# The intra-chunk product of a bidirectional SSD scan, computed with tokens instead of head channels on the output rows

## The chip, the cores and the metric

The kernel runs on one core of one Trainium2 chip. The metric is the device time of one execution in microseconds. All data are float32; a few constants and selections are bfloat16.

## The reference

The program is one inference step of a two-layer trunk for 128 context tokens and 256 latent tokens, model width 1024. A layer has a mixer (attention with 8 heads and, beside it, a bidirectional Mamba-2 scan with 8 heads of 64 channels), an output projection, and a mixture of 16 experts, each token going to two. The part that the change touches is the scan's output within a chunk. Cut to what matters:

```python
scores = einsum('bclhn,bcshn->bhcls', cc, bc) * decay_in
y_diag = einsum('bhcls,bcshp->bclhp', scores, x)        # x = xs * dt
y_off  = einsum('bclhn,bchpn,bhcl->bclhp', cc, states[:, :-1], exp(da_cs))
y = y_diag + y_off
# forward and backward direction, skip, gate:
y = y_f + flip(y_b) + d * xs
g = y * silu(z)
g = g * rsqrt(mean(g * g over each half of the 512 channels) + EPS) * norm_w
out = concatenate([attn, g]) @ w_out
```

A chunk is 128 tokens. The context is one chunk, the latent tokens are two. So `y_diag` is, for each of 3 token tiles, 8 heads and 2 directions, a product of a 128x128 matrix of decayed scores with a 128x64 matrix, summed over the two directions.

## The kernel before

Tokens lie in three tiles of 128 (t = 0 is the context, 1 and 2 the latent tokens). The program for each engine is written out by hand; engines meet at semaphores that only count upward. A wait holds back everything behind it on its engine. PSUM is used as eight banks of 128 x 512 float32, assigned by hand: names such as `YT_BANK, Y_BANK` (line 382) and `MIX_BANK` (line 389) say which.

The touched stage comes behind attention in each layer. TensorE walks through six phases p (lines 2064 to 2094). Phase p stands for token tile t = p // 2 and head group g = p % 2, four heads each. In a phase TensorE

- builds two matrices of decay exponents for the next phase (`decay_rows`, lines 1975 and 1977),
- does a share of the adaLN matmuls of later stages as filling work (`fill`, line 1724) in phases 0 to 3; in phase 4 it folds their rows into columns (`ada_columns`, line 1740), and in phase 5 turns the gate rows (`gate_rows`, line 1774),
- has single jobs: chunk states in phase 1, context states in phase 2, the products from carried states (`from_states`, line 2043) in phase 3, the turns described below,
- waits for VectorE's decayed scores of this phase (`s_scm`) and multiplies them (line 2091).

ScalarE turns the exponents into decays (`fall`, line 914, and `decay`, line 919), twelve in all, numbered k = 2p + d with d the direction. VectorE multiplies decay k with the masked group scores (`decayed`, line 1285) into one of four buffers of `scT`.

The product in line 2091 has `xdt` (128 source tokens x 64 channels of one head) as the stationary operand and `scT` (128 source tokens x 128 target tokens) as the moving one. Its output is turned: channels on the rows, target tokens on the columns, two heads in the two halves of the rows, the whole tile in bank 6. ScalarE copies a finished tile to SBUF (`y_copied`, line 907, behind decay 5, behind decay 9, and behind the last), TensorE turns it back with four transposes into bank 5 (`y_turned`, line 2052: tile 0 in phase 2, tile 1 in phase 4, tile 2 behind the first half of the projection of tile 0), and VectorE's `finish(t)` (lines 1288 to 1318) adds it to the skip term, adds the part from the states, gates it, takes the sums of squares, waits for POOL's reciprocal root and scales. `finish(0)` stands behind `decayed(7)`, `finish(1)` and `finish(2)` behind `decayed(11)`.

Then `mixed_transposes(t)` (line 2059) turns the gated tile, ScalarE copies it (`mixed_copied`, line 902), and the output projection multiplies it (`projected`, line 2108). The order behind the phases is: projection of tile 0, first half; turn of y tile 2; products from states for tile 2; second half; mixed transposes 1; projection of tile 1, and so on.

The weights come through a ring of six slots from SyncE's queue (line 460). A slot is filled again when its last product is done; the loads of all but two experts of a layer also wait for the order of experts that VectorE works out after the router (line 510).

Of the kernel before, what the change touches and what calls it, by code (L numbers as in the profile page):

```python
# [12 lines left out]
P = 128  # L13
# [3 lines left out]
NT = 3  # L17
H = 8
HD = 64
# [106 lines left out]
def hybrid_step(nc, x_prompt, x_sample, cache_k, cache_v, state_ssm, c, c_ctx, norm1_w, norm2_w,  # L126
# [4 lines left out]
    ALU = mybir.AluOpType  # L131
    ACT = mybir.ActivationFunctionType
# [3 lines left out]
    with ctx:  # L136
# [3 lines left out]
        def sem(name):  # L140
            return ctx.enter_context(nc.semaphore(name))
# [10 lines left out]
        xpad = sb("xpad", XM * 512)  # L152
# [13 lines left out]
        halves += [rot_flat[:, i * 256:(i + 1) * 256] for i in range(5)] + [xdt_rest[:, :]]  # L166
        xdt = lambda d, t, g: halves[2 * (2 * t + d) + g]
        xw = [xpad[:, i * 512:(i + 1) * 512] for i in range(4)]
        yT = (xpad[:, 0:512], xpad[:, 512:1024], scT[:, 0, :])
        b_tok = xpad[:, 4 * 512:4 * 512 + NT * P].rearrange("p (t c) -> p t c", t=NT)  # L170
        cs_rest = xpad[:, 0:2 * P].rearrange("p (d c) -> p d c", d=2)
        cs_parts = ctx.enter_context(nc.sbuf_tensor("cs_parts", [P, 2, P], bf16))
# [147 lines left out]
        s_sto, s_stoc, s_yoff, s_cdec, s_cst, s_dexp, s_scm, s_y = (sem(n) for n in (  # L320
            "state_out_transposed", "state_out_copied", "yoff_mm", "decay_sums", "cs_transposed", "decay_exp",
            "decay_scores", "y_mm"))
        s_yTc, s_ytr = sem("yT_copied"), sem("y_turned")
        s_brows = sem("bada_rows_landed")
        s_yv, s_gss, s_grs, s_ssd = (sem(n) for n in (
            "y_skip_made", "gated_sumsq", "gated_rstd", "ssd_done"))
# [52 lines left out]

        STATES = ((0, 0), (1, 0), (0, 1), (1, 2))  # L380
        YOFF_BANK = (3, 4)
        YT_BANK, Y_BANK = 6, 5
        logits = bank[7][:, 128:128 + NT * E]
        router_part = work[:, 2, 0:NT * P].rearrange("p (t c) -> p t c", t=NT)
        router_exp = work[:, 3, 0:NT * E]
# [2 lines left out]
        HEADS = (0, 4, 1, 5, 2, 6, 3, 7)  # L388
        pair_of = lambda v: v.rearrange("p (a j) -> p j a", a=2)
        ADA_BANK = 7  # L390
        MIX_BANK = (0, 6, 6)
        EXPS = 1 + 2 * H
        G_BANK = (0, 6)
        g_psum = lambda g: bank[G_BANK[g]][:, 0:NT * P]
# [352 lines left out]
        def _(act):  # L747
# [78 lines left out]
            for l in range(DEPTH):  # L826
# [72 lines left out]
                def mixed_copied(t):  # L899

                    act.wait_ge(s_mt, NT * l + t + 1)
                    act.activation(xs_tok[:, t, :], bank[MIX_BANK[t]][:, :], ACT.Copy).then_inc(s_mA, 1)

                def y_copied(t):

                    act.wait_ge(s_y, 6 * l + 2 * t + 2)
                    act.activation(yT[t], bank[YT_BANK][:, :], ACT.Copy).then_inc(s_yTc, 1)

                def fall(k):

                    act.wait_ge(s_cdec, 12 * l + k + 1)
# [17 lines left out]
                for k in range(1, 12):  # L929
                    if k < 11:  # L930
                        fall(k + 1)
                    decay(k)
                    if k in (5, 9):
                        y_copied((k - 5) // 4)
                    if k == 7:
                        act.wait_ge(s_sto, l + 1)
                        act.activation(st_out, bank[0][:, :], ACT.Copy).then_inc(s_stoc, 1)
                        act.wait_ge(s_stoc, l + 1)
                        for d in range(2):
                            for jj in range(2):  # L940
                                dma(new_state[0, l, d].rearrange("(g j hh) p n -> j (hh p) g n", g=2, j=2)[jj],
                                    st_out.rearrange("p (d j g n) -> p d j g n", d=2, j=2, g=2)[:, d, jj]
                                    ).then_inc(s_out, 16)
                    if k == 8:
                        ada_rows(l + 2)
                mixed_copied(0)
                y_copied(2)
                gates_stored(l)
                gates_loaded(l)
                mixed_copied(1)  # L950
# [93 lines left out]
        def _(dve):  # L1044
            n = [0]

            def step(ins):

                n[0] += 1
                ins.then_inc(s_dve, 1)  # L1050
                dve.wait_ge(s_dve, n[0])
# [74 lines left out]
            for l in range(DEPTH):  # L1126
# [161 lines left out]
                def finish(t):  # L1288

                    v = xs_tok[:, t, :]  # L1290
                    dve.wait_ge(s_yv, NT * l + t + 1)
                    dve.wait_ge(s_ytr, NT * l + t + 1)
                    step(dve.tensor_tensor(v, v, bank[Y_BANK][:, :], ALU.add))
                    if t:
                        dve.wait_ge(s_yoff, 4 * l + 2 * t)
                        for g in range(2):
                            for d in range(2):
                                ins = dve.tensor_tensor(heads(work[:, g, d * 256:(d + 1) * 256], 4),
                                                        heads(bank[YOFF_BANK[g]][:, d * 256:(d + 1) * 256], 4),
                                                        bc(ecs[:, d, t, 4 * g:4 * g + 4], HD), ALU.mult)  # L1300
                        step(ins)
                        for d in range(2):
                            step(dve.tensor_tensor(heads(v, 2), heads(v, 2), work[:, 0:2, d * 256:(d + 1) * 256],
                                                   ALU.add))
                    z = mixed[:, t, 512:1024]
                    step(dve.tensor_tensor(z, v, z, ALU.mult))
                    for g in range(2):
                        zg = z[:, g * 256:(g + 1) * 256]
                        ins = dve.tensor_tensor_reduce(out=work[:, 0, g * 256:(g + 1) * 256], in0=zg, in1=zg, scale=1.0,
                                                       scalar=0.0, op0=ALU.mult, op1=ALU.add,  # L1310
                                                       accum_out=gss[:, t, g:g + 1])
                    ins.then_inc(s_gss, 1)
                    dve.wait_ge(s_grs, NT * l + t + 1)
                    for g in range(2):
                        zg = z[:, g * 256:(g + 1) * 256]
                        ins = dve.scalar_tensor_tensor(out=zg, in0=zg, scalar=grs[:, t, g:g + 1],
                                                       in1=snw[:, g * 256:(g + 1) * 256],
                                                       op0=ALU.mult, op1=ALU.mult)
                    ins.then_inc(s_ssd, 1)

                for k in range(12):
                    decayed(k)
                    if k == 3:
                        next_states()
                        dve.wait_ge(s_snw, 16 * (l + 1))
                    if k == 10:
                        modulation(l + 2)
                    if k == 7:
                        finish(0)
                finish(1)  # L1330
                finish(2)
# [368 lines left out]
        def _(pe):  # L1700
# [34 lines left out]
            def ada_columns(i):  # L1735

                n = 2 * (ADA_CUT[i] - (0, *ADA_CUT)[i])
                pe.wait_ge(s_row, i + 1)
                for blk in range(ADA_BLK):
                    last = mm(bank[ADA_BANK][:, n * blk:n * (blk + 1)], ada_part[:, blk * P:(blk + 1) * P],  # L1740
                              fold[:, 0:n], start=True, stop=True)
                last.then_inc(s_rowT, 1)
# [46 lines left out]
            for l in range(DEPTH):  # L1789
# [254 lines left out]
                                      s[r, d, :], start=True, stop=True)  # L2044
                        last.then_inc(s_yoff, 1)

                def y_turned(t):

                    pe.wait_ge(s_yTc, NT * l + t + 1)
                    pe.wait_ge(s_gss, NT * l + t) if t else pe.wait_ge(s_attn, NT * (l + 1))  # L2050
                    for m in range(4):
                        last = tr(bank[Y_BANK][:, m * P:(m + 1) * P], yT[t][:, m * P:(m + 1) * P], ident[:, :])
                    last.then_inc(s_ytr, 1)

                def mixed_transposes(t):

                    pe.wait_ge(s_ssd, NT * l + t + 1)
# [6 lines left out]
                for p in range(6):  # L2064
                    if p < 5:
                        decay_rows(2 * p + 2)
                        decay_rows(2 * p + 3)
                    t, g = p // 2, p % 2
                    if p < 4:
                        fill(l, F2 + (F3 - F2) * (p + 1) // 4)  # L2070
                    elif p == 4:
                        ada_columns(l + 2)
                    else:
                        gate_rows(l)
                        pe.wait_ge(s_stoc, l + 1)
                        mixed_transposes(0)
                    if p == 1:
                        chunk_states()
                    if p == 2:
                        context_states()  # L2080
                    if p == 3:
                        pe.wait_ge(s_snx, l + 1)
                        from_states(1)
                    if p in (2, 4):
                        y_turned(t - 1)
                    pe.wait_ge(s_scm, 12 * l + 2 * p + 2)
                    for j in range(2):
                        for d in range(2):
                            for i in range(2):
                                h = 2 * j + i  # L2090
                                last = mm(bank[YT_BANK][i * HD:(i + 1) * HD, (2 * g + j) * P:(2 * g + j + 1) * P],
                                          xdt(d, t, g)[:, h * HD:(h + 1) * HD],
                                          scT[:, (2 * p + d) % 4, h * P:(h + 1) * P], start=d == 0, stop=d == 1)
                    last.then_inc(s_y, 1)


# [44 lines left out]
                if l == 0:  # L2141
                    pe.wait_ge(s_small, 16 * sum(SMALL))
                projected(0, 0)
                y_turned(2)
                from_states(2)
                projected(0, 1)
                mixed_transposes(1)
# [219 lines left out]
```

## Time and profile before

| what | value |
|---|---|
| median of 3 runs | 802.25 us (801.22 to 804.03) |
| the profiled execution's own time | 801.22 us |
| its span, first to last instruction | 799.5 us |
| TensorE matmul (PE) busy | 743.1 us, 93% |
| TensorE weight load (PEld) busy | 374.4 us, 47% |
| VectorE (DVE) busy | 328.9 us, 41% |
| ScalarE (ACT) busy | 216.1 us, 27% |
| GpSimd (POOL) busy | 142.9 us, 18% |
| bytes moved by DMA | 211.56 MB, mean 265 GB/s |
| products of line 2091 | 192 matmul records, 192 load records |
| turns of line 2052 | 24 transposes of 128x128 |

[...] A float32 matmul leaves two load and two matmul records, a float32 transpose one of each. [...] Times in a row with a count (x8) run from the first start to the last end of the group. "issue" as a releaser means that the profile shows nothing that the engine waited for. PEclk is the granted clock of TensorE as a share of full speed.

### The profile page before, as it was taken

The numbers are of one execution on the slowest core, as the hardware profiler recorded it, in microseconds if no ns is written. First come the engines' busy times: TensorE is split into PE (matmuls) and PEld (weight loads), VectorE is DVE, ScalarE is ACT, GpSimd is POOL, SyncE is SP. The second block draws the span as 40 slices with busy tenths as digits, with TensorE's granted clock in tenths as the row PEclk, the third lists the DMA queues.
The fourth block names the chain that finished last, engine by engine and source line by source line (L and its number), as shares of the span: only waits on it lengthen the run. The fifth ranks groups of instructions, "written<-read, shape, count | busy, mean of one in ns | idle before, by whom it ended". The sixth has DMA issues, their size and how long they took to land. (4 is left out here: it accounts for less than half of the span.)

```text
span 799.5 us, 9607 instructions
## 1 busy us (share of the span) xinstructions
PE 743.1 (93%) x3542; PEld 374.4 (47%) x3542; DVE 328.9 (41%) x870; ACT 216.1 (27%) x491; POOL 142.9 (18%) x238
## 2 busy tenths in 40 slices
PE   3999998999998999999899999888999899999994
PEld 1456653545446444443344755344544654444331
DVE  2023534735536453212272252564643744331136
ACT  2210255734023110111312025493411311101121
POOL 4146041120010200000112404122000120000102
PEclk9999999999999999999999999999999999999998
DMA  8997228899601999999897233345420399999961
GB/s 321 387 342 250 95 106 295 308 362 403 240 0 80 374 392 420 421 424 423 312 389 245 88 105 112 108 170 228 155 105 1 121 420 377 418 425 422 422 241 79
DMA packets 66340, 211.56 MB, mean 265 GB/s; under 512 B 7883, under 2 KB 8755, under 8 KB 54003
## 3 DMA queue, kind: packets, MB, share of 16 engines
q1 hardware_dynamic: 52744, 179.33, 57.9%
q10 hardware_dynamic: 7851, 17.70, 5.8%
q0 software_dynamic: 5696, 13.89, 4.8%
q8 instruction: 29, 0.48, 0.2%
q14 instruction: 20, 0.16, 0.1%
HBM read 202.02 MB, written 13.93 MB: 270 GB/s over the span
## 5 line engine op out<-in xcount | busy, mean ns | idle before, releaser
L2212 PE MATMUL bank<-ring,work 128*64 128x512 f32 (+1 forms) x512 | 156.5, 596 | 4.1 <-DMA ring<-in_w_up_dram 3.2
L2212 PEld LDWEIGHTS bank<-ring,work 128*64 128x64 f32 (+1 forms) x512 | 58.6, 157 | 96.2 <-issue 94.6
L2228 PE MATMUL bank<-ring,xs_tok 128*64 128x512 f32 (+1 forms) x256 | 79.9, 597 | 2.5 <-DVE xs_tok L1567 1.4
L1567 DVE COPY xs_tok<-bank 128x256 f32<-128x256 f32 x22 | 9.3, 425 | 150.7 <-PE bank L2219 150.7
L1850 PE MATMUL bank<-hT,ring 128*128 128x384 f32 x192 | 62.2, 486 | 0.0
L1724 PE MATMUL bank<-ring,cpad 128*32 128x512 f32 x384 | 48.6, 632 | 6.2 <-DMA ring<-in_w_ada_dram 5.4
L1850 PEld LDWEIGHTS bank<-hT,ring 128*128 128x128 f32 x192 | 36.5, 190 | 25.0
L2228 PEld LDWEIGHTS bank<-ring,xs_tok 128*64 128x64 f32 (+1 forms) x256 | 28.3, 157 | 39.6 <-issue 36.9
L984 ACT ACTIVATE xs_tok<-bank 128x256 f32<-128x256 f32 x22 | 8.5, 386 | 138.4 <-PE bank L2212 138.4
L2108 PE MATMUL bank<-ring,xn 128*128 128x512 f32 x96 | 43.6, 597 | 0.0
L991 ACT ACTIVATE qkv<-bank 128x512 f32<-128x512 f32 x40 | 21.7, 595 | 80.0 <-PE bank L2228 80.0
L2108 PE MATMUL bank<-ring,xs_tok 128*128 128x512 f32 x96 | 43.2, 592 | 0.0
L1795 PE MATMUL bank<-ring,hT 128*128 128x512 f32 x96 | 42.8, 597 | 0.4 <-ACT hT L797 0.4
L1907 PE MATMUL bank<-ring,hT 128*128 128x512 f32 x96 | 42.3, 593 | 0.0
L707 POOL DMA_INDIRECT hT<-h_rows,idx x18 | 18.4, 1024 | 124.0 <-PE bank L2202 77.1
L1556 DVE COPY work<-bank 128x512 f32<-128x512 f32 x42 | 27.1, 686 | 10.9 <-PE bank L2202 10.9
L1164 DVE SCALAR_TENSOR_TENSOR conv<-xpad,prm,conv 128x388 f32<-128x388 f32 x48 | 29.9, 623 | 1.7
L2108 PEld LDWEIGHTS bank<-ring,xs_tok 128*128 128x128 f32 x96 | 18.2, 190 | 23.0 <-issue 23.0
L1795 PEld LDWEIGHTS bank<-ring,hT 128*128 128x128 f32 x96 | 17.7, 190 | 22.6 <-issue 20.4
L1907 PEld LDWEIGHTS bank<-ring,hT 128*128 128x128 f32 x96 | 17.8, 190 | 20.1 <-issue 20.1
L2108 PEld LDWEIGHTS bank<-ring,xn 128*128 128x128 f32 x96 | 17.4, 190 | 19.2 <-issue 19.2
L1724 PEld LDWEIGHTS bank<-ring,cpad 128*32 128x32 f32 x384 | 10.8, 113 | 30.0 <-issue 21.7
(389 smaller groups left out, 1062.1 us busy)
## 6 DMA issues: line engine op xcount, KB each, us to landing
ring<-in_w_ada_dram SPq DMA_DIRECT2D x48, 1024.0 KB, 8.9
ring<-in_w_gate_dram SPq DMA_DIRECT2D x32, 1024.0 KB, 8.2
ring<-in_w_up_dram SPq DMA_DIRECT2D x32, 1024.0 KB, 12.3
ring<-in_w_down_dram SPq DMA_DIRECT2D x32, 1024.0 KB, 10.9
ring<-in_w_in_dram SPq DMA_DIRECT2D x16, 1024.0 KB, 14.4
ring<-in_w_out_dram SPq DMA_DIRECT2D x8, 1024.0 KB
y_exp<-qkv ACTq DMA_DIRECT2D x16, 512.0 KB, 8.1
xpad<-gate_rows ACTq DMA_DIRECT2D x6, 512.0 KB, 5.7
```

Of the source, the lines that this page charges most:

```text
L707: pool.indirect_dma_start(out=xg[b % 4], out_offset=None, in_=h_rows[:, :], in_offset=bass.IndirectOffsetOnAxis(ap=idx[:, b:b + 1], axis=0 ...
L991: act.activation(y_buf(e)[:, hf * 512:(hf + 1) * 512], bank[5 + hf][:, :], ACT.Copy).then_inc(s_yc, 1)
L1164: ins = dve.scalar_tensor_tensor(out=conv[:, m, :], in0=xpd[:, m, k:k + CONVW], scalar=tap(k), in1=conv[:, m, :], op0=ALU.mult, op1=ALU.add)
L1556: dve.tensor_copy(xgT[:, b, hf * 512:(hf + 1) * 512], bank[3 + hf][:, :]).then_inc(s_xgc, 1)
L1567: dve.tensor_copy(hidT[:, b, :], bank[2][:, 0:F]).then_inc(s_htc, 1)
L1724: last = mm(bank[ADA_BANK][ADA_TILE * q:ADA_TILE * (q + 1), :], cpad[:, c:c + ADA_TILE], slot(ADA_AT[j])[:, kt, :], start=j == a and kt < ...
L1795: last = mm(bank[t][:, :], tok(kt, t), slot(u[0])[:, kt, :], start=kt == 0, stop=kt == KT - 1)
L1850: last = mm(bank[(6 + m) % 8][:, 0:3 * P], slot(v)[:, kt, col:col + P], hT[:, kt, :], start=kt == 0, stop=kt == KT - 1)
L1907: last = mm(bank[4 + t][:, :], tok(kt, t), slot(u[3])[:, kt, :], start=kt == 0, stop=kt == KT - 1)
L2108: last = mm(bank[2 * t + hf][:, :], mixed[:, t, kt * P:(kt + 1) * P] if kt < 4 else xs_tok[:, t, (kt - 4) * P:(kt - 3) * P], slot(u + hf)[ ...
L2212: last = mm(bank[b][i * n:(i + 1) * n, :].rearrange("p (i f) -> p i f", i=2), rows_T[:, kt * P + i * n:kt * P + (i + 1) * n], gate_up_of(s ...
L2228: last = mm(bank[5 + hf][i * n:(i + 1) * n, :], hidT[:, b, f * P + i * n:f * P + (i + 1) * n], w[:, f, hf * 512:(hf + 1) * 512], start=f = ...
```

## The change

The product's operands change places: `scT` becomes the stationary operand (128x128) and `xdt` the moving one (128x64). The output then has target tokens on the rows and channels on the columns, as `finish` wants it, so the copy by ScalarE and the four transposes of each tile go, with their buffers and two semaphores. The finished tile lies in bank 6, 5 and 6 for tiles 0, 1 and 2, and `finish` reads it there. Since tile 2 uses bank 6 again, TensorE waits in phase 4 for `finish(0)`; before the products from the states of tile 2 it waits for `finish(1)`. Three things move: `finish(0)` from behind `decayed(7)` to behind `decayed(5)`, the mixed transposes of tile 0 from phase 5 to phase 4, and ScalarE's copy of them to between decay 10 and decay 11. The mixed tile 1 goes through bank 5 instead of 6.

```diff
@@ -166,7 +166,6 @@
...
         xw = [xpad[:, i * 512:(i + 1) * 512] for i in range(4)]
-        yT = (xpad[:, 0:512], xpad[:, 512:1024], scT[:, 0, :])
         b_tok = xpad[:, 4 * 512:4 * 512 + NT * P].rearrange("p (t c) -> p t c", t=NT)
@@ -320,7 +319,6 @@
...
             "decay_scores", "y_mm"))
-        s_yTc, s_ytr = sem("yT_copied"), sem("y_turned")
         s_brows = sem("bada_rows_landed")
@@ -379,7 +377,7 @@
...
         YOFF_BANK = (3, 4)
-        YT_BANK, Y_BANK = 6, 5
+        Y_BANK = (6, 5, 6)
         logits = bank[7][:, 128:128 + NT * E]
@@ -388,7 +386,7 @@
...
         ADA_BANK = 7
-        MIX_BANK = (0, 6, 6)
+        MIX_BANK = (0, 5, 6)
         EXPS = 1 + 2 * H
@@ -901,11 +899,6 @@
...
 
-                def y_copied(t):
-
-                    act.wait_ge(s_y, 6 * l + 2 * t + 2)
-                    act.activation(yT[t], bank[YT_BANK][:, :], ACT.Copy).then_inc(s_yTc, 1)
-
                 def fall(k):
@@ -930,8 +923,6 @@
...
                     decay(k)
-                    if k in (5, 9):
-                        y_copied((k - 5) // 4)
                     if k == 7:
@@ -943,8 +934,8 @@
...
                         ada_rows(l + 2)
-                mixed_copied(0)
-                y_copied(2)
+                    if k == 10:
+                        mixed_copied(0)
                 gates_stored(l)
@@ -1289,8 +1280,8 @@
...
                     dve.wait_ge(s_yv, NT * l + t + 1)
-                    dve.wait_ge(s_ytr, NT * l + t + 1)
-                    step(dve.tensor_tensor(v, v, bank[Y_BANK][:, :], ALU.add))
+                    dve.wait_ge(s_y, 6 * l + 2 * t + 2)
+                    step(dve.tensor_tensor(v, v, bank[Y_BANK[t]][:, :], ALU.add))
                     if t:
@@ -1325,7 +1316,7 @@
...
                         modulation(l + 2)
-                    if k == 7:
+                    if k == 5:
                         finish(0)
@@ -2044,14 +2035,6 @@
...
 
-                def y_turned(t):
-
-                    pe.wait_ge(s_yTc, NT * l + t + 1)
-                    pe.wait_ge(s_gss, NT * l + t) if t else pe.wait_ge(s_attn, NT * (l + 1))
-                    for m in range(4):
-                        last = tr(bank[Y_BANK][:, m * P:(m + 1) * P], yT[t][:, m * P:(m + 1) * P], ident[:, :])
-                    last.then_inc(s_ytr, 1)
-
                 def mixed_transposes(t):
@@ -2070,10 +2053,10 @@
...
                         ada_columns(l + 2)
+                        pe.wait_ge(s_stoc, l + 1)
+                        mixed_transposes(0)
                     else:
                         gate_rows(l)
-                        pe.wait_ge(s_stoc, l + 1)
-                        mixed_transposes(0)
                     if p == 1:
@@ -2081,16 +2064,15 @@
...
                         from_states(1)
-                    if p in (2, 4):
-                        y_turned(t - 1)
+                    if p == 4:
+                        pe.wait_ge(s_gss, NT * l + 1)
                     pe.wait_ge(s_scm, 12 * l + 2 * p + 2)
-                    for j in range(2):
+                    for h in range(4):
+                        hh = 4 * g + h
                         for d in range(2):
-                            for i in range(2):
-                                h = 2 * j + i
-                                last = mm(bank[YT_BANK][i * HD:(i + 1) * HD, (2 * g + j) * P:(2 * g + j + 1) * P],
-                                          xdt(d, t, g)[:, h * HD:(h + 1) * HD],
-                                          scT[:, (2 * p + d) % 4, h * P:(h + 1) * P], start=d == 0, stop=d == 1)
+                            last = mm(bank[Y_BANK[t]][:, hh * HD:(hh + 1) * HD],
+                                      scT[:, (2 * p + d) % 4, h * P:(h + 1) * P],
+                                      xdt(d, t, g)[:, h * HD:(h + 1) * HD], start=d == 0, stop=d == 1)
                     last.then_inc(s_y, 1)
@@ -2141,7 +2123,7 @@
...
                 projected(0, 0)
-                y_turned(2)
+                pe.wait_ge(s_gss, NT * l + 2)
                 from_states(2)
```

## Rows read from the trace of the kernel before

**Rows 1.** Busy time by stretch: us, busy and count by engine, clock, DMA.
```profile
166.98:197.74 30.76, 29.94 (x313) 16.26 (x309) 14.94 (x34) 13.79 (x26) 0.89 (x2) 1.00 1.05 394
197.74:232.00 34.26, 34.26 (x102) 16.50 (x101) 18.12 (x40) 6.21 (x16) 3.80 (x10) 1.00 0.43 166
543.00:573.70 30.70, 28.30 (x291) 16.79 (x287) 16.06 (x35) 14.72 (x28) 5.20 (x9) 1.00 0.57 215
```

**Rows 2.** TensorE in order of time, layer 0: start, us, instruction, count, idle before.
```profile
171.54 1.09 PE L2091 MATMUL bank<-qkv,conv 128*64 128x128 f32 x16
172.57 0.39 PE L1975 MATMUL bank<-head_of,cs_parts 128*128 128x512 bf16 x1
...
183.20 0.60 PE L2052 MATMUL bank<-ident,xpad 128*128 128x128 f32 x4
...
191.40 0.39 PE L1975 MATMUL bank<-head_of,cs_parts 128*128 128x512 bf16 x1
...
192.29 1.03 PE L1740 MATMUL bank<-fold,qT 128*128 128x28 f32 x8
193.71 0.66 PE L2052 MATMUL bank<-ident,xpad 128*128 128x128 f32 x4 [0.39 <-ACT xpad L907]
194.30 1.09 PE L2091 MATMUL bank<-qkv,rot 128*64 128x128 f32 x16
195.82 0.49 PE L1774 MATMUL bank<-ident,modT 128*16 128x128 f32 x3 [0.43 <-DVE modT L1086]
...
197.74 3.70 PE L2108 MATMUL bank<-ring,xn 128*128 128x512 f32 x8
...
204.71 0.60 PE L2052 MATMUL bank<-ident,qkv 128*128 128x128 f32 x4
205.24 1.13 PE L2043 MATMUL bank<-hT,conv 64*128 64x256 f32 x7
```

**Rows 3.** TensorE's weight loads in order of time, layer 0, same columns.
```profile
23.94 0.97 PEld L1740 LDWEIGHTS bank<-fold,qT 128*128 128x128 f32 x8 [0.55 <-issue]
...
192.24 0.97 PEld L1740 LDWEIGHTS bank<-fold,qT 128*128 128x128 f32 x8
...
194.29 0.85 PEld L2091 LDWEIGHTS bank<-qkv,rot 128*64 128x64 f32 x16 [0.17 <-issue]
```

**Rows 4.** Durations (min/median/max ns) and shapes by line; the last row in order of time.
```profile
L1740 PE MATMUL bank<-fold,qT x32: 244/256/280, 24.0 to 569.1; 128*128 128x4 f32 x16, 128*128 128x28 f32 x8, 128*128 128x12 f32 x8
L1888 PE MATMUL bank<-da,one x4: 275/282/289, 114.9 to 497.7; 128*128 128x48 f32 x4
...
497.59 0.40 PE L1888 MATMUL bank<-da,one 128*128 128x48 f32 x2
```

**Rows 5.** ScalarE and then VectorE in order of time, phases 3 to 5, layer 0.
```profile
193.07 0.59 ACT L907 ACTIVATE xpad<-bank 128x512 f32<-128x512 f32 x1
...
194.54 0.64 ACT L919 ACTIVATE xpad<-xpad 128x512 f32<-128x512 f32 x1
...
186.56 0.69 DVE L1285 TENSOR_TENSOR qkv<-qT,hT 128x512 f32<-128x512 f32 x1 [4.42 <-ACT qT L919]
...
190.49 0.88 DVE L1316 SCALAR_TENSOR_TENSOR xn<-xn,grs,qT 128x256 f32<-128x256 f32 x2 [1.10 <-POOL grs L699]
...
195.98 0.69 DVE L1285 TENSOR_TENSOR qkv<-xpad,hT 128x512 f32<-128x512 f32 x1
```

**Rows 6.** Waits of TensorE and of the weight queue: us in total, times, longest.
```profile
PE bank L2212 <- DMA ring<-in_w_up_dram: 3.2, 2, 1.8
...
PE bank L2202 <- DMA hT<-h_rows,idx: 2.8, 2, 1.6
...
SPq L510 <- DVE qT L1436: 145.9, 2, 74.5
```

**Rows 7.** Busy time by stretch ahead of and in the clock's dip, layer 1.
```profile
510.00:514.00 4.00, 1.93 (x10) 0.85 (x10) 3.08 (x14) 4.00 (x20) 2.31 (x4) 1.00 0.73 275
514.00:518.00 4.00, 4.00 (x20) 0.62 (x18) 1.17 (x5) 1.28 (x4) 0.19 (x1) 0.57 0.00 0
```

## The prediction, made before the changed kernel was run

> **What bounds the kernel now.** I read the views in this order: the table of busy times, the busy times by stretch, the order of work on TensorE inside the touched stretch, the weight loads there, ScalarE and VectorE over the same time, and the waits behind it. The table has PE busy for 93% of the span and no other engine over 41%. The touched code lies in two stretches, one a layer: the six phases of the chunk scan, and the output projection behind them. In layer 0 PE is busy 29.94 of 30.76 us in the scan and every us of the projection; in layer 1 28.30 of 30.70 [rows 1]. So TensorE's own instruction stream sets the time here, and each edit is priced first as PE time and only then as a wait taken away. In phases 0 to 3 PE never waits for another engine in layer 0 (the ada matmuls fill it). Only phases 4 and 5 show waits: PE stands before the turn of token tile 1 until ScalarE's copy is there (193.71, 0.39 idle, longer with its load), before the gate rows until VectorE has modT (195.82) [rows 2].
>
> **What stands in a phase, and what replaces it.** A phase has 8 products. In f32 each is two load and matmul records, so 16 records. Now a record loads 64 columns of xdt and streams 128 columns of scT, and two neighbours lie in the two column halves of the array: the 16 records go by in pairs. Start to start, phase 0 and the decay rows behind it lie 172.57 - 171.54 = 1.03 apart [rows 2], of which 0.17 is the handover at the semaphore (the idle time shown before a phase's first load [rows 3]): 0.86 us for 16 records.
>
> The change swaps the roles. A record then loads 128 columns of scT and streams 64 of xdt, with the whole array in use, so nothing runs in pairs. The stream is short: the four transposes of 128 columns take 0.60 with the last one's own 0.27 in it, 0.11 each [rows 2], so 64 columns are some 0.055. What counts is the load. The nearest rows are the ada columns, f32, loads of 128 columns with a short stream behind each: eight loads in 0.97 with 28 columns streamed, and eight in 0.97 with 4 [rows 3, 4]. The last load is 0.19, so the step is (0.97 - 0.19) / 7 = 0.111, and it does not depend on the stream. Two stream lengths with one step say that the load sets the pace and the stream hides beneath it. I take 0.111 for 64 columns too.
> A phase is then 16 x 0.111 = 1.78 instead of 0.86: **+0.92 us**, twelve times in the kernel.
>
> [...]
>
> Bounds of this price. From below: 0.055 a record, if the load cost nothing beside the stream, which makes a phase 0.88, as now. From above: the one row with more than 28 streamed columns, the two records of 48 columns, lies 0.40 from first start to last end, 0.275 the shorter one's own, so 0.12 to 0.13 apart [rows 4]; drawn on from 28 over 48 to 64 columns that is 0.138 a record, +0.43 a phase. Load and stream fully in series (0.166) is excluded by 4 and 28 columns costing alike. I take 0.111, since eight loads there are a longer row than two records.
>
> **Phases 0 to 3.** PE has no slack, so 4 x 0.92 = +3.68 a layer. The turn of tile 0 goes from phase 2: the four transposes at 183.20, 0.11 each, -0.44 [rows 2]; the handover before the phase stays. ScalarE loses the copy before it (0.59 for the one of tile 1 [rows 5]), which nobody else waited for. VectorE's finish of tile 0 moves from behind decay product 7 to behind product 5: 4.1 us of VectorE's time, from product 7's end at 187.25 to 191.37, with a wait for POOL inside, are then ahead of products 6 and 7. They are needed by phase 3 only, and now VectorE stands idle for 4.42 us just before product 7, so it is hidden [rows 5]. Without that cover phase 3 would wait up to 4 us. Layer 1 has the same: +3.68 - 0.44.
>
> **Phases 4 and 5, layer 0.** Now from 191.40 to 197.74, 6.34 us [rows 2]. Written out anew on PE: decay rows and ada columns as now, to 192.29 + 8 x 0.11 = 193.18, so 1.78; handover 0.17; the transposes of the mixed tile 0, moved here from phase 5, 0.44; handover 0.17; the products 1.78; handover 0.17; gate rows 0.33 (three turns at 0.11); handover 0.17; the products 1.78; handover 0.17. Sum 6.96, **+0.62**. The turn of tile 1 with its wait is gone (193.18 to 194.30), which pays for part of the two longer phases.
> Does a new wait open? What could be late is decay product 11 on VectorE, now done at 196.67, behind ScalarE's copy at 193.07 and its last exponential at 194.54 [rows 5]. ScalarE loses the copy at 193.07 (0.5 in the queue) and gains the copy of the mixed tile between the last two exponentials (0.5), ahead of the decay that product 11 needs; so that exponential stays near 194.6 to 195.2. VectorE then has the modulation before product 11, which moves up with product 10 as far as ScalarE's lost copy lets it (0.5), and so ends product 11 near 196.1. PE asks for it at 191.40 + 6.96 - 1.95 = 196.4. No wait, with 0.3 to spare. The gate rows, asked for near 195.9, find modT ready: it was 195.8 and is 0.5 earlier.
> The wait for finish 0 to have read its bank, new at phase 4, is met 4 us earlier; what would queue behind it is all of PE. In layer 1 the same comes to about +0.5, since only one gate row is turned there.
>
> **The projection.** The turn of tile 2, 204.71 to 205.24, goes: -0.5 [rows 2]. The wait in its place (finish 1's sums) is met some 3 us before PE comes to it. VectorE gets its add for tile 2 early, which helps nobody: PE works on without a gap [rows 1].
>
> **Sum.** Layer 0: 3.68 - 0.44 + 0.62 - 0.5 = 3.36. Layer 1: 3.68 - 0.44 + 0.5 - 0.5 = 3.24. Together +6.6 us. What lies behind follows PE: the queue of weights has issued all that it can and waits for the expert order (145.9 us in two waits [rows 6]), so later routing makes later loads. The profiled execution took 801.22 us (span 799.5), and so 807.8. The median of the three runs is 1.0 above it; I forecast halfway between, **808.3 us**.
>
> **Rivals.**
> (1) The load hides under the stream, or is fetched ahead: the phase stays near 0.87 us. For it: the mixed pairs of today do load ahead. Against it: the eight loads in 0.97. Then only the turns and their waits go: 0.44, in phases 4 and 5 what decay product 11 allows (PE could start phase 5 at 196.3, done at 197.4, -0.3), and 0.5: 1.3 a layer, 2.6 in all, from the same halfway base of 801.7: 799.1. This is the faster case; it decides at a step under some 0.068 us a record, where 12 x 16 x (step - 0.054) equals 2.6. [...]
> (2) The load and a stream of 64 columns overlap only in part, 0.138 a record: 12 x 0.43 = 5.2 more, 813.5. For it: the two records of 48 columns. Against: their starts may be drawn late by the record.
> (3) PE is late, but later waits for transfers take it up: PE waits 3.2 for the up weights and 2.8 for gathered rows in the expert stages [rows 6], 6.0 in all, which would leave +0.6: 802.3. Against: these transfers are themselves released by PE's results, so they move with it.
> Beside these the granted clock: it falls to 0.57 over 514 to 518 of the attention of layer 1, after PE had been busy only 1.93 of the 4 us before [rows 7]. That is the low one of its two levels for 3.4 us, worth 1.7 us; a shifted schedule may lose it or gain another. It widens the range and carries no sign.
>
> **From cases to numbers.** Forecast as summed 0.67 (own range 806 to 811); rival 2 0.13; rival 3 0.10; rival 1 0.10. A change of this kernel under 0.3% (2.4 us) can't be told from none. Slower by more: 0.80 (the first two); within: 0.10 (rival 3); faster: 0.10 (rival 1). The range 803.5 to 814.5 holds forecast and rival 2 with the clock's 1.7, and the near part of rival 3.
>
> **What would show it.** In the profile after: 16 loads of 128x128 in some 1.86 us where 16 of 128x64 took 0.85, start to start 0.11; no transposes left of the turns; the stretch from the first decay rows to the projection longer by 3.9 in layer 0; no wait of PE for ScalarE's copy or for modT; PE still without a gap over the projection. I am wrong if the loads lie 0.06 apart (rival 1), or if phase 3 or 5 opens with a wait for VectorE's decay product, which would be finish 0 or the mixed copy put in a worse place.

## The result, and the profile after

The changed kernel took 808.37 us (median of 8 runs, 804.45 to 812.98), the kernel before beside it 802.74 us (8 runs, 800.79 to 805.31). The ratio is 1.0083, with a 95% interval of 1.0062 to 1.0104: 6.7 us slower, 5.0 to 8.3. The two medians themselves lie 5.6 us apart, which is inside that interval. The forecast was 808.3 and slower.

The table of busy times of the kernel after:

```profile
PE 752.1 (93%) x3518; PEld 383.4 (47%) x3518; DVE 329.1 (41%) x870; ACT 212.5 (26%) x485; POOL 142.3 (18%) x238
```

PE is busy 9.0 us longer with 24 fewer records. The busy time by stretch answers to [rows 1]; the stretches are the same pieces of work, from the first decay rows of layer 0 to the projection, and behind it:

```profile
166.85:200.63 33.78, 33.53 (x305) 21.01 (x302) 15.74 (x36) 13.18 (x25) 0.89 (x2) 1.00 1.05 396
200.63:234.41 33.78, 33.78 (x98) 15.95 (x98) 17.12 (x38) 5.25 (x14) 3.81 (x10) 1.00 0.36 130
```

The scan took 33.78 us instead of 30.76, and PE is busy 99% of it instead of 97%. PE in order of time, as [rows 2]:

```profile
171.40 2.00 PE L2073 MATMUL bank<-conv,qkv 128*128 128x64 f32 x16
173.24 0.38 PE L1966 MATMUL bank<-head_of,cs_parts 128*128 128x512 bf16 x1
...
184.81 0.33 PE L2073 MATMUL bank<-conv,qkv 128*128 128x64 f32 x2
...
193.99 0.38 PE L1966 MATMUL bank<-head_of,cs_parts 128*128 128x512 bf16 x1
...
194.87 1.03 PE L1731 MATMUL bank<-fold,qT 128*128 128x28 f32 x8
195.73 0.64 PE L2042 MATMUL bank<-ident,xn 128*128 128x128 f32 x4
196.61 1.97 PE L2073 MATMUL bank<-rot,qkv 128*128 128x64 f32 x16 [0.24 <-DVE qkv L1276]
198.42 0.49 PE L1765 MATMUL bank<-ident,modT 128*16 128x128 f32 x3
...
200.63 3.65 PE L2090 MATMUL bank<-ring,xn 128*128 128x512 f32 x8
...
207.65 1.14 PE L2034 MATMUL bank<-hT,conv 64*128 64x256 f32 x8
```

The first pair of rows is phase 0: 1.84 us from the product to the next decay rows, where it was 1.03. Phases 1 to 3 of layer 0 grew by 0.85, 0.70 and 0.82 us. There is no turn ahead of the product at 184.81 any more. In phase 4 the fold of the ada rows, the transposes of the mixed tile and the product follow one another, with 0.24 us of waiting for VectorE's decay product of that phase; the gate rows find modT ready. Behind the first half of the projection (200.63) the products from the states come at once.

The weight loads, as [rows 3]:

```profile
171.40 1.86 PEld L2073 LDWEIGHTS bank<-conv,qkv 128*128 128x128 f32 x16 [0.84 <-issue]
...
194.81 0.97 PEld L1731 LDWEIGHTS bank<-fold,qT 128*128 128x128 f32 x8
```

Sixteen loads in 1.86 us, the last one 0.19: (1.86 - 0.19) / 15 = 0.111 each, the same step as in the ada columns below it, with 64 columns streamed instead of 28. The pace is read from starts here: the matmul records of the product are 0.275 us long by the median and start 0.11 apart. The records start one at a time now: 0.03 and 0.09 us after the start of phase 0's first load, one load has started (the first itself), where in the kernel before it is two and then four. This is the loss of the pairs of which the prediction speaks. Before, the second pair's loads (four started by 171.61) stand some 0.11 us ahead of its matmul records (two started until 171.69, four by 171.72).

### The profile page after: what moved, and what is told of

Same layout as the page of the kernel before. It is cut to its first block and busy times, and to the rows that moved or that the text cites. A ratio compares the mean times of both kernels' runs of the same rounds, so it can differ in the third digit from the quotient of the medians.

```text
span 807.8 us, 9549 instructions
## 1 busy us (share of the span) xinstructions
PE 752.1 (93%) x3518; PEld 383.4 (47%) x3518; DVE 329.1 (41%) x870; ACT 212.5 (26%) x485; POOL 142.3 (18%) x238
## 5 line engine op out<-in xcount | busy, mean ns | idle before, releaser
L2194 PE MATMUL bank<-ring,work 128*64 128x512 f32 (+1 forms) x512 | 159.7, 606 | 3.5 <-DMA ring<-in_w_up_dram 2.6
L1715 PEld LDWEIGHTS bank<-ring,cpad 128*32 128x32 f32 x384 | 10.7, 112 | 29.6 <-issue 21.7
```

Of the source, the lines that this page charges most:

```text
L1715: last = mm(bank[ADA_BANK][ADA_TILE * q:ADA_TILE * (q + 1), :], cpad[:, c:c + ADA_TILE], slot(ADA_AT[j])[:, kt, :], start=j == a and kt < ...
L2194: last = mm(bank[b][i * n:(i + 1) * n, :].rearrange("p (i f) -> p i f", i=2), rows_T[:, kt * P + i * n:kt * P + (i + 1) * n], gate_up_of(s ...
```

## The experiments

The kernel before ran beside each of them. Since the differences are a few us and single runs of one kernel spread over 6 to 8, each ratio has its interval. In the traces I compare, in each layer, the time from the first decay rows to the first product from the states (scan, first half of the projection, turn of tile 2) with the same time in the kernel before. For the changed kernel it is longer by 3.03 - 0.48 = 2.55 us in layer 0 and 2.76 - 0.50 = 2.26 in layer 1, +4.8 together. The first figure of each pair is the scan, the second the stretch behind it. The spans of the two traces lie 8.3 us apart (807.8 against 799.5), so 3.5 us of that stand outside the touched stretches; the mean granted clocks of the two are 0.989 and 0.994.

**e1, the swap undone and all else kept.** The changed kernel, with the product of before writing into the new banks:

```diff
-                            last = mm(bank[Y_BANK[t]][:, hh * HD:(hh + 1) * HD],
-                                      scT[:, (2 * p + d) % 4, h * P:(h + 1) * P],
-                                      xdt(d, t, g)[:, h * HD:(h + 1) * HD], ...)
+                                last = mm(bank[Y_BANK[t]][i * HD:(i + 1) * HD, (2 * g + j) * P:(2 * g + j + 1) * P],
+                                          xdt(d, t, g)[:, h * HD:(h + 1) * HD],
+                                          scT[:, (2 * p + d) % 4, h * P:(h + 1) * P], ...)
```

> The changed kernel with the product of before in it (64 loaded columns, 128 streamed, in pairs of column halves), so that only the swap is undone while copies and turns stay away and the moved steps stay moved. What it leaves out: the tile of y reaches the gate turned, so the values behind it are not the reference's. Theory A (the load of 128 columns is what made the change slow): without it the change is a gain; the six phases are 1.03 us each again, and against before 2.6 us are gained, up to 4 if the shorter ScalarE queue lets phases 4 and 5 start earlier: 798.5 to 800 beside a before of 802.5. Rival R (the moved steps, or the new waits for finish, cost the time): slower than before by 2 us or more here too.

Measured: 802.96 us beside 803.58, ratio 0.998 (0.9958 to 1.0002). The phase is as before, on PE in order of time:

```profile
171.60 1.09 PE L2074 MATMUL bank<-qkv,conv 128*64 128x128 f32 x16
172.63 0.39 PE L1966 MATMUL bank<-head_of,cs_parts 128*128 128x512 bf16 x1
```

In the traces the touched stretches are shorter by 1.4 us in layer 0 and 1.2 in layer 1, 2.6 together. The run times show 1.6 us, less than theory A's 2.6 to 4, with an interval that holds 2.6 and just reaches none. So no cost of the moved steps and the new waits shows, the turns were worth what the prediction's first rival gives them, and the swap makes the change slow. The routed tokens differ here, so what lies behind the scan is not compared, and the traces of the touched stretches say more than the run times.

**e2, the swap alone.** The kernel before, its product swapped, the copies and turns kept:

```diff
+                            last = mm(bank[YT_BANK][:, hh * HD:(hh + 1) * HD],
+                                      scT[:, (2 * p + d) % 4, h * P:(h + 1) * P],
+                                      xdt(d, t, g)[:, h * HD:(h + 1) * HD], ...)
...
-                    step(dve.tensor_tensor(v, v, bank[Y_BANK][:, :], ALU.add))
+                    step(dve.tensor_tensor(v, v, yT[t], ALU.add))
```

> The kernel before with the swapped product alone; copy, turns and all places stay as they were, and finish reads ScalarE's copy while the turned tile goes unused. Theory A: a phase grows by 0.81 us (1.84 against 1.03 in the traces), twelve of them 9.7, of which the waits of phases 4 and 5 take up about 1 us a layer: 7.5 to 9.5 us slower than before, slower than the whole change (which is 6.7 slower). Rival R: under 4 us slower.

Measured: 813.02 us beside 803.58, ratio 1.0119 (1.0077 to 1.0161), 9.4 us. In the traces +3.9 and +5.2 us in the two layers, 9.1. Layer 1's part holds a stretch at the lower clock, by stretch with the columns of [rows 1]:

```profile
540.00:557.60 17.60, 14.36 (x117) 8.81 (x117) 7.87 (x13) 8.39 (x17) 5.62 (x9) 1.00 0.53 187
557.70:561.00 3.30, 3.30 (x20) 2.12 (x22) 0.23 (x1) 1.38 (x3) 0.00 (x0) 0.50 0.83 350
```

PEclk is 0.50 over some 3.4 us, with PE busy all through; that is worth 1.7 us (half its length, an estimate), and 7.4 is left for the swap. PE in phase 4 of layer 0, the turn and the product:

```profile
197.16 0.66 PE L2052 MATMUL bank<-ident,xpad 128*128 128x128 f32 x4 [0.39 <-ACT xpad L907]
197.65 1.90 PE L2090 MATMUL bank<-rot,qkv 128*128 128x64 f32 x16
```

The turn still waits 0.39 us for ScalarE's copy, and the long product stands behind it. The parts add up: swap +7.4 and all the rest -2.6 make +4.8, which is what the traces of the whole change show.

**e4, the stream doubled.** The changed kernel, with 128 columns streamed in 12 of 16 records:

```diff
-                    for h in range(4):
+                    for h in reversed(range(4)):
+                        w = min(h, 1)
...
-                            last = mm(bank[Y_BANK[t]][:, hh * HD:(hh + 1) * HD], ...
-                                      xdt(d, t, g)[:, h * HD:(h + 1) * HD], ...)
+                            last = mm(bank[Y_BANK[t]][:, (hh - w) * HD:(hh + 1) * HD], ...
+                                      xdt(d, t, g)[:, (h - w) * HD:(h + 1) * HD], ...)
```

> The changed kernel with the stream doubled to 128 columns in 12 of the 16 records of a phase; the columns streamed too many are overwritten by the product behind. Theory A (load 0.112 a record, a stream of up to 128 columns hides under it): records still 0.11 apart, time within 1.5 us of the changed kernel's. Rival S (load and stream in series, or the stream sets the pace): 12 x 0.055 us a phase more, 7.9 us above the changed kernel's.

Measured: 809.14 us beside 803.58, ratio 1.0059 (1.0038 to 1.008). Its phase 0, on PE in order of time:

```profile
171.87 2.00 PE L2074 MATMUL bank<-conv,qkv 128*128 128x128 f32 x16
173.71 0.38 PE L1966 MATMUL bank<-head_of,cs_parts 128*128 128x512 bf16 x1
```

It takes 1.84 us, as with half the stream. Streams of 128 columns under these full-width f32 loads cost nothing here; rival S is out. By the medians the kernel is within 0.8 us of the changed kernel's 808.37, by the ratios 1.9 us below it, which the intervals don't tell from none.

**e3, the load cut into column halves.** The changed kernel again, each product as two, each for 64 of the 128 target tokens, in the two column halves of the array:

```diff
-                            last = mm(bank[Y_BANK[t]][:, hh * HD:(hh + 1) * HD],
-                                      scT[:, (2 * p + d) % 4, h * P:(h + 1) * P], ...
+                            for i in range(2):
+                                last = mm(bank[Y_BANK[t]][i * HD:(i + 1) * HD, hh * HD:(hh + 1) * HD],
+                                          scT[:, (2 * p + d) % 4, h * P + i * HD:h * P + (i + 1) * HD], ...
```

> The changed kernel with each swapped product cut in two: 64 columns of scT loaded into one column half, 64 into the other, 64 streamed over each; 32 records a phase, the same columns loaded in all. Theory A (columns loaded follow one another at 0.85 ns each whatever half they go to, and the stream hides): a phase stays near 1.8 us and the time within 1.5 us of the changed kernel's. Rival P (what was lost is the pairing of the column halves; in halves again, both load and stream at once): records go by in pairs at 0.06, a phase near 1.0 us, and the time 8 to 10 us below the changed kernel's. Rival O (a fixed 0.11 us a record): a phase of 3.6 us, 20 us above it.

Measured: 801.37 us beside 803.58, ratio 0.9968 (0.9947 to 0.999), 2.6 us by the ratio and 2.1 in the traces. Phase 0 on PE, and its weight loads:

```profile
173.52 1.15 PE L2074 MATMUL bank<-conv,qkv 128*64 128x64 f32 x32
174.60 0.39 PE L1966 MATMUL bank<-head_of,cs_parts 128*128 128x512 bf16 x1
```

```profile
173.52 1.01 PEld L2074 LDWEIGHTS bank<-conv,qkv 128*64 128x64 f32 x32 [0.84 <-issue]
```

My theory A fell here, in the point of why: there are 32 records instead of 16 with the same columns loaded in all, and the phase is 1.08 us instead of 1.84. The theory's 0.85 ns a column lies between the 0.84 of the kernel before (0.86 us for 16 records of 64 columns) and the 0.87 of the changed kernel (0.111 us for 128). Here the loads lie some 0.03 apart, 1.01 for all, which is 0.44 ns a column ((1.01 - 0.14) / 31 = 0.028 for 64). So the number of columns loaded does not set the pace by itself. The loads start in pairs, as in the kernel before: 0.03 us after the start of the first, two have started, 0.09 us after it four, and the pairs lie (1.01 - 0.14) / 15 = 0.058 apart. Rival P was right: the ratios place this kernel 9.2 us below the changed one, and it had 8 to 10.

**e5, the same records in another order.** All products of the one half first, then all of the other:

```diff
-                    for h in range(4):
-                        hh = 4 * g + h
-                        for d in range(2):
-                            for i in range(2):
+                    for i in range(2):
+                        for h in range(4):
+                            hh = 4 * g + h
+                            for d in range(2):
```

> The kernel of e3_half_loads (64 columns of scT loaded into one column half of the array, 64 into the other) with the same 32 records in another order: first all products of the one half, then all of the other. Theory N (only neighbours in different halves run at once): records follow one another at some 0.055 us, a phase of 1.75 to 1.9 us as in the changed kernel, and the time is the changed kernel's within 1.5 us, 7 us above e3's. Rival W (a smaller load is cheap by itself): the phase stays near 1.0 us and the time near e3's, 2.6 us below before.

Measured: 807.22 us beside 803.08, ratio 1.0042 (1.0022 to 1.0063). The weight loads of phase 0, and the one behind it:

```profile
173.40 1.76 PEld L2074 LDWEIGHTS bank<-conv,qkv 128*64 128x64 f32 x32 [0.84 <-issue]
175.23 0.10 PEld L1966 LDWEIGHTS bank<-head_of,cs_parts 128*128 128x128 bf16 x1
```

32 loads in 1.76 us, (1.76 - 0.14) / 31 = 0.052 apart on average; from the first load to the next decay rows 1.83, as in the changed kernel (1.84). One half at a time, two loads of 64 columns cost what one of 128 does, 1.76 us for the loads of the phase against 1.86. Of the two orders, only the one with neighbours in different halves starts its loads in pairs: 0.03 and 0.09 us after the start of the first load of phase 0, two and then four have started in e3, one and then two here. The time came out a little beyond theory N's bounds: 1.8 us below the changed kernel beside it by the medians where N allowed 1.5, and 5.9 above e3 by the ratios where N had 7. The traces place +2.7 and +2.4 us in the two layers, the changed kernel's figures within 0.2.

**The changed kernel once more,** beside e5:

> The changed kernel once more, beside the kernel before and three others, for the split of its loss. The two traces place +4.7 us in the touched stretches (+2.4 and +2.3), the first comparison measured 6.7. Theory A: the difference is the granted clock, which falls to its lower level for 3.4 us at a time at places that differ from run to run; time multiplied by mean clock then differs from before by 4.7 +- 0.7 us, and the raw medians by 5 to 7. Rival L: the load-bound phases cost more in runs than the trace shows; time multiplied by clock differs by over 6 us.

Measured: 809.01 us beside 803.08, ratio 1.0069 (1.0049 to 1.009). Time multiplied by mean granted clock is 801.7 us (mean of 6 runs, standard error 0.5) against 797.3 (21 runs, 0.2): 4.4 us apart. In the earlier comparison it is 802.0 for the changed kernel (35 runs) and, on the next occasion, 797.3 before (28 runs): 4.7. Both agree with the 4.8 that the first pair of traces places in the touched stretches, and rival L is out. The product of time and clock takes the whole time to follow the clock, so it is an estimate. By it the remaining 1 to 2 us of the raw difference lie in the clock, whose mean is 0.9907 to 0.9908 after and 0.9918 to 0.9923 before: 0.13% of 803 is 1.1 us.

Where the clock falls differs from run to run. In this run's trace it fell inside the scan and the projection of layer 1, by stretch, with the columns of [rows 1]:

```profile
550.00:554.40 4.40, 2.91 (x30) 1.94 (x22) 1.38 (x2) 2.12 (x4) 0.00 (x0) 1.00 0.59 205
554.50:557.90 3.40, 3.40 (x20) 2.17 (x23) 0.29 (x1) 1.43 (x3) 0.00 (x0) 0.50 0.81 340
558.50:578.00 19.50, 19.22 (x174) 13.09 (x167) 10.75 (x27) 8.43 (x17) 0.88 (x2) 1.00 0.63 229
578.50:585.00 6.50, 6.50 (x23) 4.83 (x23) 5.23 (x14) 0.27 (x1) 0.89 (x2) 0.50 0.02 4
```

The clock (the column with 1.00 and 0.50) is at 0.50 over 554.5 to 557.9, after PE had stood idle 1.5 of the 4.4 us before; and again from 578.5, though PE was busy 19.22 of the 19.50 us before it. The first trace of the changed kernel has no such stretch in the scan, though PE waits the same 1.49 us there. In this trace the touched stretch of layer 0 is again 2.55 us longer than before and that of layer 1 7.2; the two stretches at the lower clock, 3.4 and 6.8 us long, account for about 5.1 of the 7.2 at half their length, an estimate.

**e7, the product in bfloat16.** scT and xdt are written as bfloat16 for this product, which reads the copies `xdt_b`:

```diff
+        scT = qkv_flat[:, 0:2 * 512].bitcast(bf16).rearrange("p (n c) -> p n c", n=4)
...
+                            last = pool.tensor_copy(xdt_b[2 * (2 * t + d) + g], xdt(d, t, g))
+                    last.then_inc(s_xdb, 1)
```

> The changed kernel with scT and xdt in bfloat16 for this product alone (GpSimd makes the copies of xdt), so its outputs are of lower precision than the reference's. Theory A (the price of the swap is the f32 load: two records of 0.112 a product): a product is one record, and the decay rows show 128x128 bf16 loads 0.056 apart, so a phase is 8 x 0.056 = 0.45 plus handover, 0.4 below the phase of before; with the turns away as well 2.6 us, and 12 x 0.4 = 4.8 less what the waits of phases 4 and 5 keep: 4 to 7 us below before. Rival O (what costs is the record of a full-width load, whatever its type): a phase near 0.9 us, 2 to 3 us below before.

Measured: 797.32 us beside 803.08, ratio 0.9923 (0.9905 to 0.9941). Phase 0:

```profile
171.49 0.41 PE L2083 MATMUL bank<-qkv 128*128 128x64 bf16 x8
171.73 0.38 PE L1975 MATMUL bank<-head_of,cs_parts 128*128 128x512 bf16 x1
```

Eight records of 128x128 loads and 64 streamed columns take 0.24 us to the next decay rows, 0.03 each, below the 0.056 I took from the decay rows, whose streams are 128 long. So theory A's phase of 0.45 was too long, and rival O's 0.9 is out: the f32 full-width load is the expensive thing, not the full width. By time multiplied by clock e7 is 10.7 us below before (786.65 against 797.34), by the medians 5.8, inside theory A's 4 to 7. The two differ because its mean clock is the lowest, 0.9867. In its trace the clock is at 0.50 in phase 5 and the projection of both layers:

```profile
192.60:194.00 1.40, 1.29 (x9) 0.91 (x10) 1.36 (x4) 0.17 (x1) 0.00 (x0) 0.50 1.04 424
567.60:574.30 6.70, 6.14 (x15) 2.93 (x16) 5.43 (x14) 0.24 (x1) 0.89 (x2) 0.50 0.01 1
```

**e8, the mixed copy put back.** e3 with one step moved:

```diff
-                    if k == 10:
-                        mixed_copied(0)
+                mixed_copied(0)
```

> The kernel of e3_half_loads with ScalarE's copy of the mixed tile 0 put back behind the last decay, since e3's trace shows PE waiting 0.25 us in phase 4 and 0.40 in phase 5 for VectorE's decay product. Theory A: the wait of phase 5 goes and 0.3 to 0.4 us a layer is gained, 0.7 in all, under what the comparison can tell: 2 to 4 us below before, e3's level. Rival C (the copy is then late for the projection): PE waits for xs_tok ahead of the projection and the gain is lost or turned.

Measured: 801.98 us beside 803.08, ratio 0.9986 (0.9968 to 1.0004). PE in phases 4 and 5 of layer 0:

```profile
195.65 1.15 PE L2073 MATMUL bank<-rot,qkv 128*64 128x64 f32 x32 [0.25 <-DVE qkv L1275]
196.94 0.50 PE L1764 MATMUL bank<-ident,modT 128*16 128x128 f32 x3
197.83 0.34 PE L2073 MATMUL bank<-rot,qkv 128*64 128x64 f32 x4 [0.40 <-DVE qkv L1275]
```

The wait of 0.40 us that I meant to remove is still there, so theory A fell; rival C's wait ahead of the projection did not come either. e8's own trace says what product 11 waited for, on ScalarE and then on VectorE:

```profile
195.67 0.63 ACT L912 ACTIVATE xpad<-xpad 128x512 f32<-128x512 f32 x1
...
195.81 0.69 DVE L1275 TENSOR_TENSOR qkv<-qT,hT 128x512 f32<-128x512 f32 x1 [0.31 <-ACT qT L912]
196.42 0.46 DVE L1076 TENSOR_TENSOR modT<-bank,bada 128x28 f32<-128x28 f32 x4
196.92 0.26 DVE L1087 SCALAR_TENSOR_TENSOR amod<-modT,prm 128x16 f32<-128x16 f32 x2
197.09 0.68 DVE L1275 TENSOR_TENSOR qkv<-xpad,hT 128x512 f32<-128x512 f32 x1
```

The decay that product 11 needs is ready at 196.30, and VectorE comes to it at 197.09, behind product 10, which had waited for ScalarE, and the modulation (modT, amod). ScalarE's copy is not on that path. What moving the modulation would give, no run here shows. e3 and e8 can't be told apart by their times.

## Why the prediction was right

**The step per load.** Forecast 0.111 from the ada columns, measured 0.111. This term carried the result, and its nearest row was the right one. Rival 2 (0.138, drawn on from the two records of 48 columns) does not hold: in e4 a phase with 128 columns streamed takes the same 1.84 us.

**The phase.** Forecast +0.92, measured 1.84 - 1.03 = +0.81. The term was mis-sized: I kept the old gap of 0.17 for the longer product, and of 1.84 us only 1.84 - 1.78 = 0.06 is left for it. For phases 0 to 3 of both layers that is 8 x 0.11 = 0.9 us too much. Where the gap went can be read in phase 2, first before and then after the change:

```profile
184.44 0.39 PE L2091 MATMUL bank<-qkv,rot 128*64 128x128 f32 x4
184.76 0.39 PE L1975 MATMUL bank<-head_of,cs_parts 128*128 128x512 bf16 x1
```

```profile
186.32 0.39 PE L2073 MATMUL bank<-rot,qkv 128*128 128x64 f32 x2
186.54 0.38 PE L1966 MATMUL bank<-head_of,cs_parts 128*128 128x512 bf16 x1
```

Before, the last four records take 0.32 us to the decay rows, where each four ahead of them take 0.22; after, the last two take 0.22 like the others. The same 0.10 stands behind the last product in e1, e3 and e5, whose loads are half as wide, and not in e4. So in these traces most of the gap that I called the handover at the semaphore is the change from half-width loads to a full-width one, which the swap takes away.

**Phases 4 and 5.** Forecast 6.96 in layer 0, measured 200.63 - 193.99 = 6.64: four gaps were shorter than the 0.17 I gave each, and phase 4 has 0.24 us of a wait for VectorE's decay product that I had not seen. Decay product 11 was done at 198.74 and PE began phase 5's product at 198.80. So the 0.3 to spare that I forecast there was not to be had. The product's first weight loads even show a wait for VectorE:

```profile
198.80 0.30 PEld L2073 LDWEIGHTS bank<-rot,qkv 128*128 128x128 f32 x2 [0.18 <-DVE qkv L1276]
```

That is the sign that I had named as speaking against me, though its 0.18 us cost no more than the gap of 0.17 that I had allowed.

**finish(0) moved up.** VectorE ran it in phase 2, behind decay product 5:

```profile
182.17 0.68 DVE L1284 TENSOR_TENSOR xs_tok<-xs_tok,bank 128x512 f32<-128x512 f32 x1
...
185.49 0.88 DVE L1307 SCALAR_TENSOR_TENSOR xn<-xn,grs,qT 128x256 f32<-128x256 f32 x2 [1.10 <-POOL grs L697]
...
188.33 0.69 DVE L1276 TENSOR_TENSOR qkv<-qT,hT 128x512 f32<-128x512 f32 x1 [1.36 <-ACT qT L912]
...
198.06 0.68 DVE L1276 TENSOR_TENSOR qkv<-xpad,hT 128x512 f32<-128x512 f32 x1
```

It starts at 182.17, its last step ends at 186.37, 4.2 us, and decay product 7 (188.33) with its 0.69 us is done at 189.02, 3.1 us before phase 3's product at 192.15. The step is hidden, as forecast.

**The turn of tile 2.** Forecast -0.5; the stretch from the projection to the products from the states went from 7.50 us to 7.02.

**The sum.** Forecast +3.4 and +3.2. The traces show +2.5 and +2.3, 4.8 together, so 1.8 too much: 1.0 in phases 0 to 3 of both layers (0.9 of it the gaps above), 0.3 in phases 4 and 5 of layer 0, and 0.5 in the same two phases of layer 1, which I had not written out. The scan of layer 0 grew by 3.0 us, where I had named 3.9 as the sign to look for. The median agreed to 0.1 us all the same, and that was luck. My 808.3 is a base of 801.7 plus 6.6; the kernel before took 802.74 beside the changed one, 1.0 more than my base, and the medians lie 5.6 apart, 1.0 less than my 6.6. The ratio's 6.7 agrees with 6.6 only because it holds some 2 us that go by the lower granted clock, a term to which I had given no sign. The forecast was right in sign and mechanism and too large in size.

**The rivals.** Rival 1's worth of the turns, 2.6 us, is what e1's traces show. The prediction named the loss of the pairs when it said that nothing runs in pairs any more, but it put the price down to the width of the load; e3 loads the same columns in alternating halves and gets rival 1's time with the swapped product. The full-width loads step at 0.111, e5's halves one after another at 0.052, e3's alternating ones at 0.03. Rival 3 fell: nothing later took the delay up. PE's waits that it counted on, 6.0 us before, are 7.8 in the trace after:

```profile
PE bank L2184 <- DMA hT<-h_rows,idx: 5.2, 4, 1.6
...
PE bank L2194 <- DMA ring<-in_w_up_dram: 2.6, 1, 2.6
```

## What to carry to other kernels

A swap of operands that leaves the multiply count alone can nearly double a product's time on PE (here 1.03 to 1.84 us a phase): count the columns loaded and ask which loads start in pairs, as in e3, and which one by one, as in e5, before counting the columns streamed. Where a float32 product is short in its stream, try splitting the stationary operand into two column halves and letting neighbouring matmuls alternate between them. Here, with streams of 64 columns, that turned a loss of 0.7 to 0.8% into a gain of 0.3% in e3 (0.1 to 0.5%); e8, which has the same product, shows 0.1%, with an interval that just reaches none. And price the gap behind a group of records from a row where loads of the same two widths follow each other.

## What the runs showed of the hardware

Loads of 64 f32 columns alternating between the column halves step at some 0.03 us (e3), in one half at 0.052 (e5), and loads of 128 columns at 0.111 (the changed kernel); a 128x64 product in bfloat16 steps at 0.03 with a load of full width (e7). The 8 float32 products of a phase leave 16 load and 16 matmul records (the changed kernel), in bfloat16 8 of each (e7), and the three float32 transposes of the gate rows leave 3. In the kernel before PE stood idle 0.43 us ahead of the gate rows (195.82) with the transposes of the mixed tile 0 queued behind them (196.15), whose tile VectorE had finished at 191.37. Going from half-width loads to a full-width one adds 0.10 us (the kernel before, e1, e3, e5). The granted clock is 1.00 or 0.50 in these traces, 0.50 for 3.4 us at a time (514.2 to 517.6 in the kernel before) or for 6.8 (the changed kernel beside e5, from 578.3), and over the last 5.3 us of the kernel before. In one trace of the changed kernel it fell to 0.50 behind a stretch in which PE had been busy 99% of 19.5 us. Its mean differs from kernel to kernel, from 0.9867 in e7 and 0.9893 in e2 to 0.993 in e5, and 0.9918 to 0.9923 before. I had not expected either, and the cause stays open.
